# A decoder layer on one TensorE-bound core: two weight splits move from GpSimd to VectorE, and the first selection drops its smallest scores instead of taking its largest

## The reference, cut to what matters

```python
h = concat(meta, x)
h = layer_norm(alpha * h + 0.5 * swiglu(h, ffn1...), ln1_g, ln1_b)
h = layer_norm(alpha * h + hybrid_mixer(h, ...), ln2_g, ln2_b)
h = layer_norm(alpha * h + 0.5 * swiglu(h, ffn2...), ln3_g, ln3_b)
return h[:, 16:]
```

```python
score = einsum('bqhs,bqh->bqs', relu(logits), w_idx)
score = where(causal, score, -inf)
_, sel = top_k(score, topk)
```

## Time and profile before

| | us |
|---|---|
| median of 3 runs | 1145.0 |
| lowest and highest | 1143.48, 1147.84 |
| the profiled execution, time | 1143.24 |
| the profiled execution, span | 1141.5 |
| PE busy in the span | 1090.9 (96%) |
| DVE busy | 487.4 (43%) |
| ACT busy | 340.5 (30%) |
| POOL busy | 148.3 (13%) |
| mean granted TensorE clock | 0.973 of full |

### The profile page before, as it was taken

The page is one execution under the profiler, slowest core; times in us unless marked ns, Lnnn a source line. Parts: engine busy times, 40 slices in busy tenths (PEclk is TensorE's granted clock), DMA queues, the critical chain, the costliest instruction groups (busy, mean ns, idle before and its releaser), DMA issues.

```text
span 1141.5 us, 16006 instructions
## 1 busy us (share of the span) xinstructions
PE 1090.9 (96%) x6569; PEld 939.0 (82%) x6569; DVE 487.4 (43%) x768; ACT 340.5 (30%) x434; POOL 148.3 (13%) x100
## 2 busy tenths in 40 slices
PE   8999999999999989998988899989999999999993
PEld 7999999999999977687865468868888888888882
DVE  4333323232222373798869442463332323223235
ACT  3322223232121243524135342252222223212211
POOL 5000000000111144234131003430000000000001
PEclk9999999999999989988998899989999999999997
DMA  6433232422233331131210001213334242152311
GB/s 188 111 94 90 79 105 73 110 62 76 79 100 101 99 95 39 37 111 38 74 42 33 1 1 37 76 46 100 100 84 110 74 110 74 59 156 77 101 51 74
DMA packets 159165, 90.34 MB, mean 79 GB/s; under 512 B 6596, under 2 KB 156792, under 8 KB 159128
## 3 DMA queue, kind: packets, MB, share of 16 engines
q1 hardware_dynamic: 159128, 89.83, 27.7%
HBM read 87.72 MB, written 2.10 MB: 79 GB/s over the span
## 4 chain that ended last, share of the span: by engine, by line
PE 85%; DVE 10%; ACT 2%; POOL 1%; issue 1%; DVEq 0%; POOLq 0%
PE ps L901 73%; PE ps L1310 3%; PE ps L1036 3%; PE ps L1290 2%; DVE qk L1599 1%; POOL xl L480 1%; PE ps L1301 1%; DVE x L1527 1%; DVE sc L1562 1%; DVE zrow L1485 1%; DVE top L1561 1%; ACT whi L610 1%; DVE sil L1517 1%; PE ps L1318 1%; DVE sil L1521 1%
## 5 line engine op out<-in xcount | busy, mean ns | idle before, releaser
L901 PE MATMUL ps<-xh,whi 128*128 128x264 f32 (+1 forms) x1264 | 357.7, 332 | 9.3 <-ACT xh L696 7.5
L901 PE MATMUL ps<-xl,whi 128*128 128x264 f32 (+1 forms) x1264 | 351.8, 330 | 3.6 <-POOL xl L480 3.3
L901 PE MATMUL ps<-xh,wlo 128*128 128x264 f32 (+1 forms) x1264 | 354.7, 330 | 0.0
L901 PEld LDWEIGHTS ps<-xh,whi 128*128 128x128 f32 x1264 | 213.5, 190 | 37.5 <-issue 12.3
L901 PEld LDWEIGHTS ps<-xl,whi 128*128 128x128 f32 x1264 | 213.6, 190 | 28.5 <-POOL xl L480 6.9
L901 PEld LDWEIGHTS ps<-xh,wlo 128*128 128x128 f32 x1264 | 214.7, 190 | 22.5 <-issue 0.2
L1385 DVE TENSOR_TENSOR wlo<-wraw,whi 128x2048 fp32r<-128x2048 f32 (+1 forms) x77 | 160.1, 2080 | 143.8 <-ACT whi L610 143.8
L610 ACT ACTIVATE whi<-wraw 128x2048 fp32r<-128x2048 f32 (+1 forms) x89 | 152.4, 1712 | 129.6 <-PE ps L901 123.6
L901 PE MATMUL ps<-hh,whi 128*128 128x264 f32 (+1 forms) x528 | 141.5, 322 | 0.0
L901 PE MATMUL ps<-hl,whi 128*128 128x264 f32 (+1 forms) x528 | 141.1, 321 | 0.0
L901 PE MATMUL ps<-hh,wlo 128*128 128x264 f32 (+1 forms) x528 | 140.4, 320 | 0.0
(11 more groups left out here) (209 smaller groups left out, 912.2 us busy)
## 6 DMA issues: line engine op xcount, KB each, us to landing
wraw<-in_ffn_w_gate SPq DMA_DIRECT2D x44, 512.0 KB, 4.0
wraw<-in_ffn_w_up SPq DMA_DIRECT2D x43, 512.0 KB, 5.2
wraw<-in_ffn_w_down SPq DMA_DIRECT2D x32, 384.0 KB, 3.4
wraw<-in_ffn_w_down SPq DMA_DIRECT2D x32, 320.0 KB, 3.9
wraw<-in_w_in SPq DMA_DIRECT2D x19, 512.0 KB, 4.6
wraw<-in_w_out SPq DMA_DIRECT2D x8, 512.0 KB, 4.0
xin<-in_x SPq DMA_DIRECT2D x2, 1024.0 KB, 5.9
out<-zrow SPq DMA_DIRECT2D x8, 256.0 KB, 2.0
```

Source lines behind the costliest of these rows:

```text
L901: mm = pe.matmul(ps[:, b + e, 0:width], w, mov, start=(first and n == 0), stop=(last and n == 2))
```

## The change

Three edits.

1. The low part of the second slot of the mixer (unit MIX0 + 1) and of the second feed-forward stage (unit UNIT0[2] + 1) is made by VectorE directly behind its normalisation, and no longer by GpSimd ahead of its share of it. GpSimd waits for the first of these before it counts unit 2.
2. Selection for query block 1 no longer takes the largest 128 in 16 rounds. It copies the negated scores in reversed order into a free buffer and, in two rounds, removes the up to 16 smallest. A table `keep8`, made by GpSimd before the first normalisation, says how many a row drops.
3. The causal mask of block 1's scores fills with a large positive value, so that masked keys are not among the smallest.

```diff
+ABSENT = 3.2e38
+DROPS = END[1] - TOPK
...
+            keep8 = sb("keep8", [P, 2, 8], F32, s)
...
 @@ gpsimd, mixer() @@
                 pool.memset(v1[:, :, :, ML_DV:VW], 1.0).then_inc(pad_ready, 1)
-                mix_lo(1)
+                link(pool.memset(keep8[:, :, :], TAKEN))
+                pool.affine_select(out=keep8[:, :, :], in_=keep8[:, :, :], compare_op=ALU.is_ge, fill=ABSENT,
+                                   base=DROPS - P, pattern=[[-8, 2], [-1, 8]], channel_multiplier=1)\
+                    .then_inc(keep_ready, 1)
                 norm_lo(0)
+                pool.wait_ge(w_lo, MIX0 + 2)
                 mix_lo(2)
                 mix_lo(3)
...
-                    pool.affine_select(out=d, in_=d, compare_op=ALU.is_ge, fill=MASKED, base=0,
+                    pool.affine_select(out=d, in_=d, compare_op=ALU.is_ge, fill=-MASKED if j == 1 else MASKED, base=0,
...
             sums(1)
-            mix_lo(MIX_UNITS + 1)
             norm_lo(1)
...
 @@ vector @@
+            def drop_lowest():
+                w = sc[:, SC_OFF[1]:SC_OFF[1] + END[1]]
+                back = sil[:, 0, 0:END[1]]
+                dve.wait_ge(idx_masked, 1)
+                dve.wait_ge(keep_ready, 1)
+                link(dve.tensor_scalar(back, w[:, ::-1], -1.0, None, ALU.mult))
+                for r in range(2):
+                    link(dve.max(top8[:, r, :], back))
+                    link(dve.tensor_tensor(top8[:, r, :], top8[:, r, :], keep8[:, r, :], ALU.max))
+                    link(dve.match_replace(back, top8[:, r, :], back, TAKEN))
+                dve.tensor_scalar(w, back[:, ::-1], (MASKED + TAKEN) / 2, UNPICKED, ALU.is_lt, ALU.mult).then_inc(bias_ready, 1)
...
             norm(0)
+            lo(MIX0 + 1, 1, UW)
             index_scores()
-            select(1)
+            drop_lowest()
             gate_rows()
...
             norm(1)
+            lo(UNIT0[2] + 1, 1, UW)
             ffn(2)
```

More of the change, by code:

```diff
@@ L245, in build @@
         idx_masked = sem("idx_masked")
+        keep_ready = sem("keep_ready")
         bias_ready = sem("bias_ready")
```

## The result

| | before | after |
|---|---|---|
| median of 5 runs each, us | 1145.0 | 1138.14 |
| lowest and highest | 1140.55, 1147.84 | 1135.61, 1140.12 |
| profiled execution: time, span | 1143.24, 1141.5 | 1135.61, 1133.9 |
| mean granted clock | 0.973 | 0.981 |

The ratio is 0.9949 [0.9926, 0.9971]: 5.8 us less, between 8.5 and 3.3. (Ratios and intervals stand here as they were measured; they are not the quotients of the two medians, which differ by 6.9 us here.) Forecast were 3.5 less and 1141.5, with a range from 1138.0 to 1146.5. The time lies in the range by 0.14 us. So the number alone shows little.

A forecast was written before the change was run, and what follows sets the result against it. TensorE, busy 96% of the span, was taken as the bound. -1.48 and -2.04 us in the normalisations and 0.0 for the selection sum to -3.5, from 1145.0 to 1141.5 us; range 1138.0 to 1146.5.

The forecast's parts named there:

- Part 1: Both normalisations: without GpSimd's split ahead, L1517 takes about 0.5 us and ends 3.05 and 3.15 us earlier.
- Part 2: Normalisation ends: VectorE's split delays GpSimd's block 7, 1.57 us in the first; nets -1.48 first, -2.04 second.
- late loads: SyncE's later loads into the slot, in mixer and second feed-forward stage: hidden, the first with some 8 us to spare.
- Part 3: First selection falls from 12.65 to some 2.6 us; 0.72 gained at the gate rows is offset at unit 4, net 0.0.
- A: Both normalisations and the gate rows: the exchange costs nothing, -6.9 us in all, 1138.1 us; chance 0.10.
- C: L1517 in both normalisations is slow by itself, so the stall stays and the returning split adds: 1147.7 us; chance 0.02.
- B: Normalisation ends: clock falls behind block 7's wait, 3.0 us each; one place 1144.5 us, chance 0.14; both 1147.5, 0.06.
- The sum: Whole kernel: -1.48 and -2.04 in the normalisations, 0.0 for the selection, -3.5 us in all, to 1141.5.

The follow-up runs named there:

- Experiment 2: The changed kernel with both splits back on GpSimd, only the first selection new; 1142.79 us, ratio 0.9981 to the kernel before.
- experiment 4: The changed kernel with each of the two splits cut into two instructions of 1024 columns; 1136.91 us, ratio 0.9939 to the kernel before.
- experiment 6: The changed kernel with a hold: the gate rows' first scan waits until unit 4's split is counted; 1138.48 us, ratio 0.9935 to before.
- splits only: The changed kernel with its two splits on VectorE but the old selection, plain mask and no `keep8`; 1139.99 us, ratio 0.9966 to before.
- experiments 5: The changed kernel run again, unchanged; 1139.24 us, ratio 0.9943 to the kernel before.
- 10: The changed kernel with splits halved, the last xl block on VectorE between halves, and the scan waiting for unit 4's split; 1136.04 us, ratio 0.9945.

## Why the prediction was right, step by step

**Part 1, the stall goes: right.** Said 0.5 for the instruction and a remaining wait of 0.6 to 0.8 for the first `xh`; measured 0.43 and 0.6. Experiment 2 brings the 3.55 back with the split, so the cause is shown. The Trainium skill, SBUF — State Buffer, section "SBUF: two separate sides", says the pair of ports that VectorE and GpSimd share is an exclusive lock: whoever starts first has it for the whole instruction. 3.55 against 0.43 and the halves of experiment 4 agree. Of operations with a single SBUF input the page counts only those in a two-port mode, and in its section "Who interferes with whom" it names `tensor_scalar` among those that can run in one; the stalled instruction is a `tensor_scalar` on float32, and the trace does not show its mode.

**Part 2, the split comes back at the end: right in size.** Block 7 late by 1.56 (2.88 for 1.32, said 1.57), a split of 3.46 (said 3.4). First normalisation -1.56, said -1.48. The working took it as settled that GpSimd, having asked first, has block 6 first; in three of six profiles with that whole split and GpSimd's blocks as in the changed kernel it did not, and the gain there is 1.35 by waits. Second -1.87, said -2.04, by another way than said: the split fell ahead of block 6, since GpSimd had lost its lead by 0.01 at the third scaling. Both late loads were hidden.

**Part 3, the selection: right by waits, short by the clock.** Selection 2.4 (said 2.6), unit 4's split 5.42 (5.4), TensorE's wait 1.0 (0.9), no wait for the gate rows, 0.0 net; experiment 6 shows the scan to be the reason. What the working left out is in the table's columns for units 5 and 6. Behind the gate rows the clock falls in every profile, but not equally long. With the wait of 0.7 ahead of it (before three times, splits only twice) the stage took 19.86, 18.14, 21.39, 18.17 and 19.84; without it, in nine profiles, 18.15 to 18.17. Windows behind the gate rows: before, before's third execution, changed.

```profile
498.00:502.00 4.00, 4.00 (x8) 1.39 (x6) 3.73 (x13) 3.36 (x6) 3.21 (x1) 0.58 0.02 4
502.00:506.00 4.00, 4.00 (x18) 3.35 (x18) 3.73 (x13) 0.00 (x0) 1.55 (x2) 0.57 0.38 98
```

```profile
502.00:506.00 4.00, 4.00 (x16) 3.15 (x15) 3.75 (x12) 0.00 (x0) 1.63 (x2) 0.50 0.34 88
506.00:510.00 4.00, 4.00 (x24) 4.00 (x23) 3.73 (x13) 0.00 (x0) 0.00 (x0) 0.64 0.51 176
```

```profile
498.00:502.00 4.00, 4.00 (x15) 2.27 (x15) 3.73 (x13) 3.98 (x6) 2.35 (x1) 0.87 0.00 0
502.00:506.00 4.00, 4.00 (x26) 4.00 (x25) 3.73 (x13) 0.13 (x1) 2.45 (x2) 0.70 0.15 20
```

The five average 19.48, 1.3 over the nine. If the two groups were the same, three long ones would all fall among the five in 10 of 364 draws. But unit 6 gives part of it back, since a second fall reaches into it, and the stage takes 22.3 to 22.7 or 23.6 to 23.7: over both columns the five average 42.42 and the nine 41.56, so 0.9 is left, and without the one execution of 45.06 it is 0.2. It points to a worth of the selection of up to 0.9 us through the clock, which the interval of experiment 2 (from 4.8 less to 0.5 more) neither excludes nor needs. It was found after the last run: no experiment was made on it, and it isn't shown.

**The rivals.** A fell: block 7, or block 6, is held up. That its 1138.1 is the measured time is luck. C fell. B was half right in its mechanism: of the five profiles with a wait of 1.6 to 2.3 before block 7 or block 6 at the end of the first normalisation (changed twice, hold, splits only twice) two show a fall behind it, none in the second normalisation, and it costs 1.2 to 1.5 us, not 3.0; the prediction sized it from the 6 us that a fall of before lasted, but here it was over sooner (windows 435 to 439 stood at 0.86 and 1.00).

**The sum: the weak step.** It took -3.5 by waits, and the waits gave -3.4 (-3.2 in the execution where the split went ahead of block 6). The two measurements say -5.8 [-8.5, -3.3] and -6.5 [-7.9, -5.3]. The first holds 3.4, only just; the second doesn't. With two fifths of 1.35 against the change and 0.9 for it, and -3.3 between the two orders, the sum would be -3.7. The prediction's sum has no term for anything outside the three places, and that is where it is short, by about 2 us, whose cause stays open.

Two things on record bear on it. First, the runs of before differ from chip to chip: their medians are 1143.07 (19 runs) and 1143.41 (32), but 1145.0 (5) and 1145.8 (11) in the two comparisons of the changed kernel. On the chip of the 1145.8 the mean granted clock of before's runs was 0.9705, on the other two 0.9722 and 0.9723, so that comparison holds some luck. Over all chips, 79 runs of before average 1143.8 and 11 of the changed kernel 1138.8, which is 5.0 less. Second, the falls of the clock elsewhere don't explain the rest: the mean granted clock of before's 62 runs is 0.972 and that of the changed kernel's 11 is 0.978. An estimate from these: 0.006 of 1140 us is some 14 us less at 1.2 GHz, and the two falls that went from the normalisations are about 6.9 each (0.57 over 8 us). Outside the normalisations the changed kernel's clock was on average no better. One candidate is the pace of the second feed-forward stage: it has two values, 360.2 and 361.3, the kernel before has shown both (361.3 once in three), the changed one 360.2 both times, and splits only, with one of the smallest gains, 361.3 both times. These counts settle nothing.

## What to carry to other kernels

Where a short VectorE instruction shows several times its usual time and ends with one of GpSimd, as here (3.55 for 0.43), suspect that the two exclude each other: move the long one behind whatever has successors, cut it into pieces, or give it to the engine that goes last. Work freed on an engine off the critical path is worth only the wait at its end, and a queue that arrives earlier may take the shared port from another (the scan, 0.8 us). A rise of the mean granted clock is not yet time: here two falls went that had stood where TensorE followed GpSimd's pace anyway. Before a profile is compared with another, find which stages no edit touches and see how much these differ: here by up to 3.9 us, more than the whole effect by waits.

## What was not expected of the hardware

The granted clock falls at different places in executions of one program: 14.43 and 15.95 for unit 1 (hold and changed, one program up to there, behind waits of 1.65 and 1.63), 99.27 and 103.47 for the attention of the changed kernel, and 18.14 to 21.39 for unit 5 in the kernel before, each time behind the wait of 0.72. Two instructions that ask within 0.02 us for the shared port may go either way, in the same program too (experiments 5 and 10), at 0.2 and 0.7 us. And at a granted clock of 1.00 throughout, dense products have two paces; their groups in the second feed-forward stage (count, busy us, mean ns) in the changed kernel, then in splits only again:

```profile
L908 PE MATMUL ps<-xl,whi 128*128 128x512 f32 x308 | 121.5, 394 | 0.0
```

```profile
L904 PE MATMUL ps<-xl,whi 128*128 128x512 f32 x313 | 124.1, 396 | 0.0
```

In the other two groups of this shape the means differ by about 1 ns, and over the some 960 products of the stage's first 222 us this is roughly the 1.1 us; what sets the pace is open.
